# Sharing the later modulation tiles of a decoder layer between VectorE and GpSimd

## The reference

```python
def modulation(c, w_mod, b_mod):              # w_mod: 2048 x 12288
    m = jax.nn.silu(c) @ w_mod + b_mod
    return jnp.split(m[:, None, :], 6, axis=-1)   # sh1, sc1, g1, sh2, sc2, g2

hm = rms_norm(x) * (1.0 + sc1) + sh1
x = x + g1 * mlstm_mixer(hm, w_in, gate_bias, h_norm, w_out)
hf = rms_norm(x) * (1.0 + sc2) + sh2
x = x + g2 * conv_ffn(hf, w_up, conv_w, conv_b, w_down)
```

## Time and profile before

| | |
|---|---|
| median of 3 runs | 1203.59 us |
| the profiled execution | 1203.7 us, span 1201.9 us |
| TensorE matmul busy | 1173.5 us (98%) |
| VectorE busy | 916.7 us (76%) |
| ScalarE busy | 627.4 us (52%) |
| GpSimd busy | 147.7 us (12%) |
| granted clock of TensorE, mean | 0.983 |
| the 48 tiles at L940 | 114.6 us of VectorE, from 174.8 to 446.7 us of the span |

### The profile page before, as it was taken

The page is one execution under the profiler, slowest core; times in us unless marked ns, Lnnn a source line. Parts: engine busy times, 40 slices in busy tenths (PEclk is TensorE's granted clock), DMA queues, the critical chain, the costliest instruction groups (busy, mean ns, idle before and its releaser), DMA issues.

```text
span 1201.9 us, 17196 instructions
## 1 busy us (share of the span) xinstructions
PE 1173.5 (98%) x5922; PEld 1000.8 (83%) x5922; DVE 916.7 (76%) x992; ACT 627.4 (52%) x912; POOL 147.7 (12%) x152
## 2 busy tenths in 40 slices
PE   5799999999999999999999999999999999999998
PEld 5788888878888888888888888888888888888887
DVE  5799978789988998988887446888885446777654
ACT  4354565655654456555554445555554445555442
POOL 0000020100012210222121000212211000121100
PEclk9599999999999998999999999999999999999999
DMA  9999989899999993898885568878866566766552
GB/s 361 358 387 402 400 292 390 300 375 352 347 363 349 390 316 114 245 261 233 226 249 194 193 204 244 232 214 256 230 211 208 180 204 179 195 186 184 201 165 80
DMA packets 260441, 314.56 MB, mean 262 GB/s; under 512 B 6208, under 2 KB 186888, under 8 KB 251688
## 3 DMA queue, kind: packets, MB, share of 16 engines
q1 hardware_dynamic: 259360, 312.51, 78.4%
q0 software_dynamic: 592, 1.22, 0.4%
q10 hardware_dynamic: 442, 0.21, 0.1%
HBM read 311.80 MB, written 2.11 MB: 261 GB/s over the span
## 4 chain that ended last, share of the span: by engine, by line
PE 86%; DMA 8%; DVE 3%; issue 1%; SPq 1%; ACT 0%; POOL 0%; DVEq 0%; ACTq 0%
PE ps L1231 27%; PE ps L1237 14%; PE ps L1266 9%; PE ps L1267 9%; PE ps L1268 9%; DMA m<-in_l_w_mod_dram 7%; PE ps L1313 4%; PE ps L1314 4%; PE ps L1315 4%; DVE acc L967 1%; DMA mod_raw<-in_l_w_mod_dram 1%; PE ps L1336 1%; SPq L342 1%; DVE acc L940 1%; PE ps L1341 1%
## 5 line engine op out<-in xcount | busy, mean ns | idle before, releaser
L927 DVE TENSOR_TENSOR w_lo<-raw,w_hi 128x1024 fp32r<-128x1024 f32 x392 | 482.0, 1231 | 186.7 <-ACT w_hi L567 185.4
L567 ACT ACTIVATE w_hi<-raw 128x1024 fp32r<-128x1024 f32 x392 | 414.1, 1057 | 352.0 <-PE ps L1268 167.9
L1231 PE MATMUL ps<-hm,w_hi 128*128 128x512 f32 x1408 | 356.1, 393 | 1.7 <-DVE hm L1159 1.7
L1231 PEld LDWEIGHTS ps<-hm,w_hi 128*128 128x128 f32 x1408 | 253.1, 189 | 46.5 <-issue 1.9
L1237 PEld LDWEIGHTS ps<-hm,w_lo 128*128 128x128 f32 x1408 | 194.5, 191 | 15.1
L1237 PE MATMUL ps<-hm,w_lo 128*128 128x256 f32 x1408 | 198.7, 283 | 0.0
L1313 PE MATMUL ps<-w_hi,hm 128*128 128x512 f32 x384 | 156.4, 407 | 3.2 <-DVE hm L978 2.7
L1314 PE MATMUL ps<-w_lo,hm 128*128 128x512 f32 x384 | 151.9, 395 | 0.0
L1315 PE MATMUL ps<-w_hi,hm 128*128 128x512 f32 x384 | 151.7, 395 | 0.0
L1266 PE MATMUL ps<-w_hi,act_hi 128*128 128x512 f32 x344 | 134.3, 390 | 0.0
L1267 PE MATMUL ps<-w_lo,act_hi 128*128 128x512 f32 x344 | 133.9, 389 | 0.0
(11 more groups left out here) (169 smaller groups left out, 1067.4 us busy)
## 6 DMA issues: line engine op xcount, KB each, us to landing
raw<-in_l_w_up_dram SPq DMA_DIRECT2D x88, 1024.0 KB, 5.9
mod_raw<-in_l_w_mod_dram SPq DMA_DIRECT2D x56, 1024.0 KB, 6.5
raw<-in_l_w_in_dram SPq DMA_DIRECT2D x96, 512.0 KB, 8.2
raw<-in_l_w_down_dram SPq DMA_DIRECT2D x44, 1024.0 KB, 5.0
m<-in_l_w_mod_dram SPq DMA_DIRECT2D x32, 640.0 KB, 7.2
raw<-in_l_w_out_dram SPq DMA_DIRECT2D x16, 1024.0 KB, 8.7
m<-in_l_w_mod_dram SPq DMA_DIRECT2D x16, 768.0 KB, 13.2
mod_wide<-in_l_w_mod_dram SPq DMA_DIRECT2D x8, 1024.0 KB, 7.1
```

Of the source, the lines that this page charges most:

```text
L567: nc.scalar.activation(w_hi[:, v % 4, :], raw[:, v // 2 % 4, (v % 2) * HALF:(v % 2 + 1) * HALF], ACT.Copy).then_inc(w_hi_made, 1)
L927: nc.vector.tensor_tensor(w_lo[:, v % 4, :], raw[:, v // 2 % 4, (v % 2) * HALF:(v % 2 + 1) * HALF], w_hi[:, v % 4, :].bitcast(f32), ALU.su ...
L1231: mm(ps[:, 4 + w % 4, :], w_hi[:, v % 4, j * P:(j + 1) * P], both, start=(k == 0), stop=False, skip_group_check=True)
```

## The change

Of each of the 48 tiles, VectorE adds the first 1536 columns (BY_POOL = 3 * QUARTER) with the same kind of instruction. GpSimd handles the last 512 columns in two instructions. The first scales them in place by cT, with one tensor input. The second adds them to acc, with two. It waits for the first by the new semaphore mod_scaled. The end of the add counts in the new semaphore mod_last_done. Whoever waited for the sums (the loads of the next tiles, TensorE's column sums and gate rows, one ScalarE step) now waits for both semaphores.

GpSimd's program becomes a loop over the slots, which places each head, each add_y, the clearings of acc and the small transfers in a slot, with the tiles of that slot behind them. GpSimd reaches a tile as soon as what stands ahead of it in its own program is done and the tile has landed; it does not wait for VectorE's part. The setting of ones_row is moved to the start, and the clearing of acc for the last chunk is moved from behind add_y to slot V_OUT + 12.

```diff
+    BY_POOL = 3 * QUARTER
@@ SyncE, load_mod
                 elif MOD_WIDE + 4 <= k < 3 * KT:
                     sp.wait_ge(mod_done, k - 1)
+                    sp.wait_ge(mod_last_done, k - 3)
                 else:
                     sp.wait_ge(mod_done, plus + k + 1)
+                    wait_from_1(sp, mod_last_done, k - 1)
@@ GpSimd
+            def add_mod_last(k):
+                chunk, tile = divmod(MODS_ALONE + k, KT)
+                src, landed, count = mod_place(k)
+                pool.wait_ge(acc_ready[chunk % 2], 16 * (chunk // 2))
+                pool.wait_ge(landed, 16 * count)
+                scaled = src[:, BY_POOL:D]
+                nc.gpsimd.tensor_scalar(scaled, scaled, cT[:, tile:tile + 1], None, ALU.mult)\
+                         .then_inc(mod_scaled, 1)
+                pool.wait_ge(mod_scaled, k + 1)
+                wait_from_1(pool, mod_last_done, k)
+                part = acc[:, chunk % 2, BY_POOL:D]
+                nc.gpsimd.tensor_tensor(part, part, scaled, ALU.add).then_inc(mod_last_done, 1)
...
+            for p in range(V_PASS1, V_OUT + 31):
+                e, f = p - V_VO, p - V_OUT
+                if e == 2:
+                    pool.wait_ge(m_made, 1)
+                    pool.dma_start(m_rows_d[:, :], m_row[:]).then_inc(m_out, 16)
+                if e == 3:
+                    pool.wait_ge(m_out, 16)
+                    for h in range(H):
+                        pool.dma_start(m_bc[h][:], m_rows_d[h, :].partition_broadcast(P))\
+                            .then_inc(m_bc_in[h], 16)
+                h = head_at(e, E_PV + 2)
+                if h is not None:
+                    head(h)
...
+                if f in (14, 16, 24):
+                    add_y((14, 16, 24).index(f))
+                if f == 12:
+                    pool.wait_ge(colsum_done, 10)
+                    clear_acc(5)
+                add_due_mods(p)
@@ VectorE, add_mod
-                part = acc[:, chunk % 2, :]
-                nc.vector.scalar_tensor_tensor(out=part, in0=src,
+                part = acc[:, chunk % 2, 0:BY_POOL]
+                nc.vector.scalar_tensor_tensor(out=part, in0=src[:, 0:BY_POOL],
@@ TensorE, at each use of a chunk's sums (and the same once on ScalarE)
                 pe.wait_ge(mod_done, 2 + 3 * KT)
+                pe.wait_ge(mod_last_done, 3 * KT)
```

More of the change, by code:

```diff
@@ L200, in hybrid_mlstm_convffn_adaln_kernel @@
         wide_in = [sem(f"wide_in{s}") for s in range(2)]
-        mod_done = sem("mod_done")
+        mod_done, mod_scaled, mod_last_done = sem("mod_done"), sem("mod_scaled"), sem("mod_last_done")
         acc_cleared = sem("acc_cleared")
@@ L411, in load_g2 @@
                 sp.wait_ge(mod_done, 2 + 3 * KT + tile + plus)
+                sp.wait_ge(mod_last_done, 3 * KT)
                 sp.sem_inc(sp_began, 1)
@@ L469, in _ @@
             nc.gpsimd.memset(minus_half, -0.5).then_inc(consts_made, 1)
+            nc.gpsimd.memset(ones_row[:], 1.0).then_inc(consts_made, 1)
             def clear_acc(n):
@@ L508, in _, with add_due_mods @@
             nc.gpsimd.memset(v[:, :, :, DV], 1.0).then_inc(v_ones, 1)
[L510 to L522, removed]
+            def add_mod_last(k):
[10 more added lines that the diff above has]
+                nc.gpsimd.tensor_tensor(part, part, scaled, ALU.add).then_inc(mod_last_done, 1)
+            def add_due_mods(p):
+                for k in range(3 * KT):
+                    if MOD_SLOT[k] == p:
+                        add_mod_last(k)
             def add_y(i):
@@ L527, in add_y @@
                     pool.wait_ge(y_scaled, 4 + 2 * i + t + 1)
-                    part = x[:, t, ds(i * QUARTER, QUARTER)]
+                    part = x[:, t, i * QUARTER:(i + 1) * QUARTER]
                     nc.gpsimd.tensor_tensor(part, part, y_tmp[:, t, :], ALU.add).then_inc(x_added, 1)
[L531 to L537, removed]
+            pool.wait_ge(params_made, 1)
+            for p in range(V_PASS1, V_OUT + 31):
[11 more added lines that the diff above has]
+                    head(h)
+                if e == E_GATE + 3 * E_HEAD + 1:
+                    pool.wait_ge(g_summed, 4)
+                    clear_acc(4)
+                if f == 14:
+                    for t in range(TB):
+                        pool.wait_ge(x_in[t], 32)
+                    nc.gpsimd.memset(ss_quarter[:, :, 4], EPS).then_inc(eps_set, 1)
+                if f in (14, 16, 24):
[4 more added lines that the diff above has]
+                add_due_mods(p)
             pool.wait_ge(ss_summed, 1)
@@ L818, in take_z @@
                     act.wait_ge(mod_done, 2 + 3 * KT)
+                    act.wait_ge(mod_last_done, 3 * KT)
                 for j in range(4):
@@ L1452, in attend @@
                     pe.wait_ge(mod_done, 2 + KT)
+                    pe.wait_ge(mod_last_done, KT)
                     pe.wait_ge(probs_made, b + 3)
@@ L1508, in _ @@
                             pe.wait_ge(mod_done, 2 + 2 * KT)
+                            pe.wait_ge(mod_last_done, 2 * KT)
                             pe.wait_ge(g_copied, 4)
```

## The result

The changed kernel takes 1229.64 us in the median of 4 runs (1229.28 to 1234.45). The kernel before, in runs beside it, takes 1204.28. The ratio is 1.0222, with a 95% interval of 1.0207 to 1.0236, so the change costs 25.4 us. Forecast were +12, and a range up to 1231. The sign and the stretches were right; the size was not, and a part of the cause was missing. The kernel's profiled execution took 1234.45 us (span 1232.2), 4.8 above the median, so its trace shows more loss (span +30.3) than the medians do: of the eight executions of this kernel, here and in e5, five took 1228.03 to 1229.97 us and three 1233.51 to 1234.45, and the two that were traced are among the three.

The account below looks back on a forecast made before the run. TensorE, busy for 98% of the span, was taken to bound the kernel, with VectorE next. Terms of 4.7 (heads' turns), 4 (start of the heads) and 3 (the rest) made +12 us on 1203.7, forecast 1215.6; range 1204 to 1231.

Parts of the forecast that it names:

- The port: Each tile: GpSimd's reads block VectorE, 0.48 us by the scaling and 1.04 by the add, 1.52 together at most.
- The share of the holds that counts: Each tile: three quarters of the holds, 1.15 us, cost VectorE time; less 0.53 saved, net +0.62 us.
- The failing step: Ends of chunks: TensorE's added waits cost nothing, since GpSimd doesn't wait for VectorE's part and is only 12% busy.
- The start of the heads: 229 to 270 us: a tile load starts about 2 us later and the 2.45 us stall grows; +4 us.
- The rest: 355 to 456 us: 14 tiles' net work less VectorE's idle time and slack, +3 us; before 229 us, nothing.
- The turns themselves: Heads, 275 to 355 us: each turn 18.2 us against 16.94, five turns less the slack once, +4.7 us.
- the slack of 1.8 us: Heads' turns: VectorE has `gated` ready 1.8 us before TensorE transposes it, taken once off the five turns' loss.
- The relief: Rival: ahead of the first head, VectorE's 0.53 us gain on five tiles removes the 2.45 us stall; 1199.5 us; 10%.
- The absorbed case: Rival: holds cost about 0.8 us a tile and the heads' slack covers them; 1203.7 us, give or take 2; 13%.
- The loads rival: GpSimd ends its part late, so the tiles' two-buffer circuit sets the pace: +18 over 24 tiles, 1228 us; 15%.
- The rule of the Trainium skill: Port blocked for the whole recorded instruction: up to 1.93 us a tile, net +1.40; weighed against shorter holds in the rows.
- What was to show: Predicted signs: VectorE over 97% busy from 275 to 450 us, TensorE waiting for `gated`, nothing changed after 475 us.

Follow-up runs that it names:

- e5: The changed kernel run once more, unaltered, with a second trace; 1231.25 us, ratio 1.0213 to the kernel before.
- e6_constant: The changed kernel, with GpSimd scaling by a constant (0.5, plus 0.0) instead of a number for each partition; 1219.84 us, ratio 1.0124.
- e8_free_loads: The changed kernel, with GpSimd scaling and adding within acc alone, so no tile load waits for it; last 512 columns' sums left out; 1217.68 us.
- e15_free_constant: The changed kernel, with GpSimd working within acc alone (no load waits for it) and scaling by a constant; last 512 columns' sums left out; 1209.7 us.
- e16_free_all: e15_free_constant with the six adds to x also moved from GpSimd to VectorE; 1206.21 us, ratio 1.0021.
- e7_memsets: The changed kernel, with seven GpSimd memsets of 512 columns instead of scaling and add, waits kept, those columns' sums left out; 1205.63 us.
- e11: The changed kernel with GpSimd's share halved to 256 columns of each of the 48 tiles; 1213.51 us, ratio 1.0082.
- e3: The changed kernel, with GpSimd taking its part only of tiles 9 to 32, those in the heads' slots; 1215.76 us, ratio 1.0108.
- e9: The changed kernel, with GpSimd skipping its part of tiles 9 and 10 (those columns left out); 1228.95 us, ratio 1.0217.
- e4: The changed kernel, with GpSimd taking its part only of tiles 33 to 47, those beside w_out; 1216.11 us, ratio 1.0106.
- e14: e4 with the six adds to x made by VectorE instead of GpSimd; 1211.48 us, ratio 1.0057.
- e1: The kernel before, with VectorE adding only the first 1536 columns of the tiles and nobody the last 512; 1200.78 us, ratio 0.998.
- e12: The kernel before, with slot V_VO + 11 emptied, V_VO + 39 filled and the tiles between moved to the next tile slot; 1200.14 us.

## Why the prediction was right in sign and wrong in size

**The port, right.** VectorE around 300 us in the changed kernel, and GpSimd beside it:

```profile
300.38 2.32 DVE L959 TENSOR_TENSOR w_lo<-raw,w_hi 128x1024 fp32r<-128x1024 f32 x1
302.62 2.24 DVE L972 SCALAR_TENSOR_TENSOR acc<-mod_raw,cT,acc 128x1536 f32<-128x1536 f32 x1
304.78 2.32 DVE L959 TENSOR_TENSOR w_lo<-raw,w_hi 128x1024 fp32r<-128x1024 f32 x1
...
308.94 2.84 DVE L972 SCALAR_TENSOR_TENSOR acc<-mod_raw,cT,acc 128x1536 f32<-128x1536 f32 x1
```

```profile
299.00 2.61 POOL L528 TENSOR_TENSOR acc<-acc,mod_raw 128x512 f32<-128x512 f32 x1
301.59 2.54 POOL L523 TENSOR_SCALAR mod_raw<-mod_raw,cT 128x512 f32<-128x512 f32 x1
304.21 1.80 POOL L528 TENSOR_TENSOR acc<-acc,mod_raw 128x512 f32<-128x512 f32 x1
```

The two engines take turns. The reader is to subtract the undisturbed lengths: 2.32 - 1.22 = 1.10 us behind an add, 2.24 - 1.81 = 0.43 behind a scaling, and 2.84 - 1.81 = 1.03 behind an add again. The forecast had 1.04 and 0.48. The minimum of L972 is 1.80 (forecast 1.81), its mean 2.11 (above 2.1), and L959 between 275 and 350 us has a mean of 1.68 where I named 1.5 or so.

**The share of the holds that counts, nearly right.** From the mean of both instructions between 280 and 350 us, a tile's charge is (tile - 1.81) plus (w_lo - 1.22) times the number of `w_lo` for each tile, counted in that stretch. The turn is the usual one behind the first. In us:

```
kernel              w_lo   tile   w_lo/tile  charge  less 0.53   turn
changed             1.689  2.296  19/12      1.23    +0.70       18.69
e6_constant         1.534  2.308  20/12      1.02    +0.49       17.92
e8_free_loads       1.566  2.212  20/12      0.98    +0.45       17.93
e15_free_constant   1.399  2.298  21/13      0.78    +0.25       17.2
e16_free_all        1.379  2.308  21/12      0.78    +0.25       16.95
e7_memsets          1.226  1.811  21/12      0.01    -0.52       16.96
```

The forecast took 1.15 and +0.62, so +1.3 a turn; the kernel has 1.23, +0.70 and +1.75 (18.69 against 16.94). The table says more: the turn grows with VectorE's net time, from about +0.25 a tile on. It is not all of it: e15 and e16 have the same net and differ by 0.25 us, and e11, with +0.15 by the same sum, has 17.5. And the charge is no property of the port alone. Two instructions of the same width cost VectorE 0.78 us a tile when GpSimd's part is short and no load waits for it, and 1.23 when it is long and loads do. I read it so: the longer GpSimd's part takes, the more of its reads stand against an instruction of VectorE, and each of them makes GpSimd longer in turn. The numbers fit, but it is not shown: no run varied the collisions by themselves, and e8, e15 and e16 also read other columns.

**The failing step: that GpSimd "is only 12% busy", with its scaling taken as 0.6 us and the add as 1.3.** I priced GpSimd's part by `o_sig` and then asked only what it takes from VectorE. What it takes for itself, 4.5 us a tile and 5 beside a `mod_wide` one (3.22 + 1.80), entered two terms at 1.9:

- The start of the heads, +4 forecast, +10.35 in the trace (+8.55 in e5's). The load of 235.86 went out at 247.92, 12 us later and not 2. GpSimd's and SyncE's timelines show why, ahead of them the row's transfer as it was before the change:

```profile
228.82 0.55 POOL L513 DMA_DIRECT2D m_rows<-m_row  x1 [6.80 <-DVE m_row L1029]
```

```profile
228.73 1.57 POOL L523 TENSOR_SCALAR mod_raw<-mod_raw,cT 128x512 f32<-128x512 f32 x1 [0.89 <-DMA mod_raw<-in_l_w_mod_dram]
230.38 5.17 POOL L528 TENSOR_TENSOR acc<-acc,mod_raw 128x512 f32<-128x512 f32 x1
235.50 0.61 POOL L547 DMA_DIRECT2D m_rows<-m_row  x1
240.55 4.31 POOL L551 DMA_DIRECT2D m_bc<-m_rows  x8 [4.43 <-DMA m_rows<-m_row]
244.88 1.59 POOL L523 TENSOR_SCALAR mod_raw<-mod_raw,cT 128x512 f32<-128x512 f32 x1
246.56 1.28 POOL L528 TENSOR_TENSOR acc<-acc,mod_raw 128x512 f32<-128x512 f32 x1
```

```profile
247.92 0.34 SPq L335 DMA_DIRECT2D mod_raw<-in_l_w_mod_dram  x1
```

  The transfer of the row stands behind a scaling and an add of 5.17 us. It starts at 235.50 instead of 228.82 (`m_row` itself was ready only 1.4 us later than before), lands 3 us later than it used to after its issue (a wait of 4.43 against 1.36), and the eight small ones follow. Only then comes the tile. VectorE stood idle for 8.21 us ahead of the tile of 252.99, which starts 5.07 us after that load's issue, and its next `w_lo` is the one that TensorE waited 4.48 us for:

```profile
252.99 1.82 DVE L972 SCALAR_TENSOR_TENSOR acc<-mod_raw,cT,acc 128x1536 f32<-128x1536 f32 x1 [8.21 <-issue]
```

  e3 shows what the backlog is made of: without GpSimd's part of the first nine tiles the transfer left at 229.36, the load at 239.91, and the head was 3.3 us late, close to the +4 of the forecast. So, by these traces, what the term lacked is the lateness that the nine tiles hand on, which the prediction put at nothing since it looked only at VectorE's idle time. e9 took tiles 9 and 10 away and got back little in the medians. My estimate from the medians is that this term is less than in the traces: 25.4 - 8.15 - 11.5 leaves 5.7 us. It would fit if executions near the median lack the wait of 4.48 us, but none of them was traced, so this and the split among the causes stay open.

- The rest, +3 forecast, +11.5 in the trace and +12.1 by e4. I had named the adds to `x` as queued with the tiles and gave them nothing. GpSimd was full there, so they came late. Some 5 us hang on them (e4 against e14). The others hang on VectorE's charge and on transfers that come late, and no run parts the two.

The turns themselves, +4.7 forecast, took +8.15. Part is the net time (+1.75 for +1.3). The rest is the slack of 1.8 us, which I took off once: TensorE reached the first head already waiting, 2.45 us before and 6.24 now, so there was none to use up.

**The rivals.** The relief fell: e1 gives 3.3 us only where GpSimd does nothing, and e7, where its reads are gone, has none left. The rival had also counted too many tiles, five between 250 and 270 us: the trace before has three between 250 us and the first `gated` (at 253.76, 257.15 and 261.69), worth 1.6 us, and e1's first head came 1.55 us earlier. The absorbed case holds for e16 (+2.0), but not for this change. The loads rival, which priced a round with a scaling of 0.6 us, named the right circuit with the wrong size: 37 loads wait for GpSimd. Yet it is no cause by itself, as e7 shows, in which 37 loads wait for GpSimd too (+1), and the holds by themselves are hardly one either (e16, +2.0, at 0.78 us a tile). Together they cost 25 us. No run holds VectorE for 1.23 us a tile without the lateness, so how much of the loss lateness makes directly, and how much by way of more holds, stays open. Taking away one part of GpSimd's lateness gives about half back (e6 +15.2, e8 +13.1), both parts most of it (e15 +5.5). The forecast's frame, one price for the port and a separate check of the loads, could not show that.

The rule of the Trainium skill that the prediction weighed ("SBUF — State Buffer", section "SBUF: two separate sides") stayed too dear: by the whole recorded instruction the scaling would have held VectorE for 1.56 us, and it held 0.43, no more than the 0.48 of the short one.

**What was to show.** VectorE was to be busy for over 97% from 275 to 450 us. It was so in no stretch of the changed kernel (23.8 of 25 at the most), and what it idled for from 275 to 350 was mostly ScalarE's `w_hi`, 4.7 us. From the up stage on nothing changed, as forecast. The clock did fall behind the long stalls, to 0.86 in the stretches from 275 and from 450 us (the 0.93 from 250 us was there before), which the range had and the value had not. TensorE's new waits ended mostly with VectorE (`gated`, `w_lo`), but 5.8 us at L1519 ended with GpSimd's adds to `x`, which no step had priced.

## What to carry to other kernels

Before work goes to an idle engine, price the instruction in its exact form, operand kinds included, and follow what is already queued on that engine and what waits for the freed buffer; a share of 12% over the span says nothing of the 250 us where the work is. Where two engines exclude each other, don't take the price for a constant: here it was 0.78 us a tile with a short part on the helper and 1.23 with a long one. An experiment that takes away one of two causes can return half and hide that both are needed (e6, e8 and e15). If the engine to be relieved holds the critical one up in a single place, moving its work in time may bring what relieving it everywhere can: e12 brought 3.2 us, e1 3.3.

## What the runs showed of the chip

- A multiplication of 128 x 512 on GpSimd takes 0.62 us with a constant factor (`o_sig`, and the minimum in e6, e15 and e16) and 1.56 with a number for each partition. VectorE is held for 0.43 to 0.48 in both, so the other 1 us is no port time. It is no fixed cost either: with 256 columns the least is 0.92 (e11).
- A GpSimd instruction that finds VectorE at work can be passed more than once. The add issued at 230.38, with VectorE in its L972 from 230.33, took 5.17 us in which VectorE ran that tile and two `w_lo` undisturbed:

```profile
230.33 1.80 DVE L972 SCALAR_TENSOR_TENSOR acc<-mod_raw,cT,acc 128x1536 f32<-128x1536 f32 x1
232.06 2.34 DVE L959 TENSOR_TENSOR w_lo<-raw,w_hi 128x1024 fp32r<-128x1024 f32 x2
```

  The earlier trace rows had a case of it, 3.86 us. What decides who is passed was not found.
- A memset on GpSimd holds nothing on VectorE (e7: 1.22 and 1.81 us beside 336 memsets).
- How long the small transfer of the row is waited for goes with the other transfers in flight. In ten of the 18 traces the wait is 1.36 to 1.53 us, and there the DMA share in the 1.5 us from its issue is 0.18 at the most. In seven it is 2.94 to 4.60 us, with a share of 0.33 to 1.08; the changed kernel is one of them, where SyncE issued a tile's load 0.13 us behind it, at 235.63. e16 lies between (2.06 us, share 0.12). No run varied this by itself.
